# One row per token for the expert outputs: written by the first expert, accumulated by the second, with a last stage that reads half and gate/up weights in one transfer

## The reference, cut to what matters

```python
def hier_moe(h, w_coarse, b_coarse, w_fine, b_fine, w_gate, w_up, w_down):
    ...
    grp = jnp.argmax(pg_all, axis=-1)
    ...
    top_v, top_i = lax.top_k(fine, TOP_K)
    pe = jax.nn.softmax(top_v, axis=-1) * pg[:, None]
    ...
    a = (jax.nn.silu(jnp.einsum('td,edf->tef', t, w_gate))
         * jnp.einsum('td,edf->tef', t, w_up) * gates[:, :, None])
    y = jnp.einsum('tef,efd->td', a, w_down)
...
    x = x + g2 * hier_moe(h2, w_coarse, b_coarse, w_fine, b_fine, w_gate, w_up, w_down)
...
        y_prompt = rmsnorm(yp, final_g)
```

## Time and profile before

| | us |
|---|---|
| median of 3 runs | 995.99 (995.22 to 996.94) |
| the profiled execution | 995.4 |
| its span | 993.4 |
| stage 6, 603 to 951 us of the span | 348 |
| last stage, 951 to 993 us | 42 |

### The profile page before, as it was taken

The page is one execution under the profiler, slowest core; times in us unless marked ns, Lnnn a source line. Parts: engine busy times, 40 slices in busy tenths (PEclk is TensorE's granted clock), DMA queues, the critical chain, the costliest instruction groups (busy, mean ns, idle before and its releaser), DMA issues. The chain is left out here.

```text
span 993.4 us, 11991 instructions
## 1 busy us (share of the span) xinstructions
PE 908.7 (91%) x4615; PEld 688.2 (69%) x4615; DVE 601.5 (61%) x828; ACT 388.0 (39%) x551; POOL 158.2 (16%) x103
## 2 busy tenths in 40 slices
PE   4799999999996999978999956999999999999946
PEld 3589888999984555437888844767676777767512
DVE  6753223132424666544588774787888878788528
ACT  6431111011104766512453323655555454555114
POOL 0000000000004910000110101233233332323100
PEclk9899999999995999999999965999999999999979
DMA  9535535311002300021222183799999999999177
GB/s 371 211 120 204 202 140 218 100 44 43 1 1 90 105 1 2 8 70 43 85 64 67 61 359 130 280 379 357 374 362 366 364 363 367 361 369 342 71 286 306
DMA packets 38261, 190.95 MB, mean 192 GB/s; under 512 B 9654, under 2 KB 10806, under 8 KB 22840
## 3 DMA queue, kind: packets, MB, share of 16 engines
q1 hardware_dynamic: 28844, 170.76, 45.9%
q0 software_dynamic: 9216, 18.89, 5.0%
q10 hardware_dynamic: 144, 0.52, 0.1%
HBM read 178.48 MB, written 26.35 MB: 206 GB/s over the span
## 5 line engine op out<-in xcount | busy, mean ns | idle before, releaser
L1755 DVE TENSOR_TENSOR gu_lo<-w_gu,gu_hi 128x2048 fp32r<-128x2048 f32 x64 | 146.1, 2286 | 47.6 <-ACT gu_hi L1673 47.5
L573 PE MATMUL PS<-h_hi,w_hi 128*128 128x384 f32 x432 | 148.2, 343 | 5.4 <-DVE h_lo L436 5.4
L577 PE MATMUL PS<-h_hi,w_lo 128*128 128x384 f32 x432 | 145.1, 336 | 0.0
L575 PE MATMUL PS<-h_lo,w_hi 128*128 128x384 f32 x432 | 145.1, 336 | 0.0
L1673 ACT ACTIVATE gu_hi<-w_gu 128x2048 fp32r<-128x2048 f32 x64 | 122.0, 1907 | 19.8 <-PEq L1022 11.9
L1922 PE MATMUL PS<-gu_hi,xT_hi 128*128 128x512 f32 x256 | 116.6, 455 | 2.7 <-DVE xT_lo L1761 2.7
L1955 PE MATMUL PS<-w_d,aT 128*128 128x512 f32 x256 | 115.2, 593 | 1.3 <-DVE yrows L1783 1.3
L1622 POOL DMA_INDIRECT y_rows<-yrows,tab x32 | 69.3, 2167 | 213.9 <-DVE yrows L1783 213.9
L1924 PE MATMUL PS<-gu_hi,xT_lo 128*128 128x512 f32 x256 | 102.5, 400 | 0.0
L1923 PE MATMUL PS<-gu_lo,xT_hi 128*128 128x512 f32 x256 | 101.5, 397 | 0.0
L573 PEld LDWEIGHTS PS<-h_hi,w_hi 128*128 128x128 f32 x432 | 81.8, 189 | 14.2 <-issue 11.0
(11 more groups left out here) (200 smaller groups left out, 1523.8 us busy)
## 6 DMA issues: line engine op xcount, KB each, us to landing
w_gu<-in_w_gu SPq DMA_DIRECT2D x64, 1024.0 KB, 10.7
w_d<-in_w_down SPq DMA_DIRECT2D x32, 1024.0 KB
wm<-in_w_mod SPq DMA_DIRECT2D x10, 2048.0 KB, 8.0
w_raw<-in_w_in SPq DMA_DIRECT2D x18, 512.0 KB, 8.7
yt<-y_rows SPq DMA_DIRECT2D x9, 1024.0 KB, 13.2
xt<-in_x_all SPq DMA_DIRECT2D x9, 512.0 KB, 3.5
y_all<-yt SPq DMA_DIRECT2D x9, 512.0 KB, 2.8
wmh<-in_w_mod SPq DMA_DIRECT2D x2, 2048.0 KB
```

The source lines that it names most:

```text
L573: pe.matmul(o, w_hi[b][:, k, :], h_hi[:, k, tok], start=k == 0, stop=False)
L575: pe.matmul(o, w_hi[b][:, k, :], h_lo[:, k, tok], start=False, stop=False)
L577: last = pe.matmul(o, w_lo[b][:, k, :], h_hi[:, k, tok], start=False, stop=k == KD - 1)
L1755: dve.tensor_tensor(gu_lo[:, n % 3, h, :], w_gu[:, n % 3, h, :], raw(gu_hi[:, n % 2, h, :]), ALU.subtract).then_inc(s_lo, 1)
```

## The change

`y_rows` has one row for each token. Of a token's two experts the one that comes first in the order of processing writes its row, the other adds to it with an accumulating DMA. For this the table's entries are no longer 2 * token + k + 1 but 2 * token + 1 for the first and 2 * token + 2 for the later one; which is later is found in `slots` by comparing the experts' numbers (`chosen`, plus 32 for each round of 128 places). `split_table` makes two lists of `tab`: `tabw`, where the later ones are out of bounds, and `taba`, where the first ones are. In the last stage 0.5 MiB is loaded for each tile; tiles 1, 3, 5 and 7 are added to the residual by PE alone, with an identity matrix, and their squares and scaling read PSUM; the other five by one DVE addition. The gate/up weights of an expert come in one transfer of 2 MiB, issued after the second half's products.

```diff
+            def final_rows(t):
+                return PS[:, 2 * (t // 2):2 * (t // 2) + 2, :] if t in PE_SUMS else halves(yt[:, t, :])
...
                     for n in range(NE):
                         if n + 3 < NE:
-                            for h in range(2):
-                                sp.wait_ge(s_gu, 2 * n + h + 1)
-                                load_gu(n + 3, h)
+                            sp.wait_ge(s_gu, 2 * n + 2)
+                            load_gu(n + 3)
...
                     def scatter(n):
                         pool.wait_ge(s_y, n + 1)
                         pool.indirect_dma_start(
                             out=y_rows, out_offset=bass.IndirectOffsetOnAxis(
-                                tab[:, n:n + 1].bitcast(U32), 0),
+                                tabw[:, n:n + 1].bitcast(U32), 0),
...
+                        if n >= 1:
+                            pool.wait_ge(s_out[(n - 1) % 2], 16 * ((n - 1) // 2 + 1))
+                        pool.indirect_dma_start(
+                            out=y_rows, out_offset=bass.IndirectOffsetOnAxis(
+                                taba[:, n:n + 1].bitcast(U32), 0),
+                            in_=yrows[:, n % 2, :], in_offset=None, bounds_check=T - 1,
+                            oob_is_err=False, compute_op=ALU.add).then_inc(s_acc[n % 2], 16)
...
                     def high(n, h):
-                        act.wait_ge(s_wgu[n % 3][h], 16 * (n // 3 + 1))
+                        act.wait_ge(s_wgu[n % 3], 16 * (n // 3 + 1))
...
                     def blend(n):
                         if n >= 2:
                             dve.wait_ge(s_out[n % 2], 16 * (n // 2))
+                            dve.wait_ge(s_acc[n % 2], 16 * (n // 2))
...
+                        dve.wait_ge(s_yt[t], 16)
+                        x = yt[:, t, :].rearrange("p (k n) -> p k n", k=KD)
+                        dve.tensor_tensor(x, x, cat[:, :, t * P:(t + 1) * P], ALU.add
                                           ).then_inc(s_x3, 1)
...
                     for t in range(NT):
-                        combine(t)
+                        if t not in PE_SUMS:
+                            combine(t)
                         if t:
                             finish(t - 1)
```

More of the change, by code:

```diff
@@ L126, in build @@
         with ExitStack() as same:
-            slotf, entry, tab, tabg, gtab, of_ctx, tabacc, count, gu_lo, w_d = later_buffers(same)
+            slotf, entry, tab, tabg, gtab, tabw, taba, of_ctx, tabacc, count, gu_lo, w_d = later_buffers(same)
         with ExitStack() as same:
-            for name, shape, dt in LATER[:8]:
+            for name, shape, dt in LATER[:10]:
                 allocator(same)(name + "_y", shape, dt)
-            yt = allocator(same)("yt", [P, NT, TOPK, D])
+            yt = allocator(same)("yt", [P, NT, D])
         with ExitStack() as same:
-            for name, shape, dt in LATER[:8]:
+            for name, shape, dt in LATER[:10]:
                 allocator(same)(name + "_w", shape, dt)
@@ L969, in build @@
         s_xclear = sem("s_xclear")
-        s_wgu = [[sem(f"s_wgu{i}_{h}") for h in range(2)] for i in range(3)]
+        s_wgu = [sem(f"s_wgu{i}") for i in range(3)]
         s_wd = [sem(f"s_wd{i}") for i in range(3)]
@@ L993, in build @@
             erm = sb4("erm", [P, 2, NE])
-            cmax, csum, grp, v0, v1, ex, e01 = [sb4(f"per_tile{i}", [P, NT]) for i in range(7)]
+            cmax, csum, grp, v0, v1, ex = [sb4(f"per_tile{i}", [P, NT]) for i in range(6)]
+            chosen = sb4("chosen", [P, TOPK, NT])
+            turn_of = sb4("turn_of", [P, TOPK, 3], I32)
+            order = sb4("order", [P, TOPK, 3])
             gates = sb4("gates", [P, TOPK, NT])
@@ L1258, in choose @@
                                           ).then_inc(s_rdve, 1)
-                        for k in range(TOPK):
-                            link(dve.tensor_tensor(entry[:, k, tiles, 0, :], oh[k][:, tiles, :],
-                                                   spread(row_id[:, k, tiles], NE), ALU.mult))
                     def slots(t0, n):
@@ L1277, in slots @@
                         dve.sem_inc(s_within, 1)
+                        tiles = slice(t0, t0 + n)
+                        turns, later_of = turn_of[:, :, 0:n], order[:, :, 0:n]
+                        link(dve.tensor_copy(turns, slotf[:, :, tiles]))
+                        link(dve.tensor_scalar(turns, turns, 7, 5, ALU.logical_shift_right,
+                                               ALU.logical_shift_left))
+                        link(dve.tensor_tensor(chosen[:, :, tiles], chosen[:, :, tiles], turns,
+                                               ALU.add))
+                        for k in range(TOPK):
+                            link(dve.tensor_tensor(later_of[:, k, :], chosen[:, k, tiles],
+                                                   chosen[:, 1 - k, tiles], ALU.is_gt))
+                        link(dve.tensor_tensor(later_of, later_of, row_id[:, :, tiles], ALU.add))
+                        for k in range(TOPK):
+                            link(dve.tensor_tensor(entry[:, k, tiles, 0, :], oh[k][:, tiles, :],
+                                                   spread(later_of[:, k, :], NE), ALU.mult))
                     def weigh(t0, n):
@@ L1358, in _ @@
                                       ).then_inc(s_tab, 1)
+                    split_table(0)
                     dve.tensor_tensor(gtab[:], PS[:, 7, TABLE + NE:TABLE + 2 * NE],
@@ L1512, in build @@
         s_store = sem("s_store")
+        s_acc = [sem(f"s_acc{i}") for i in range(2)]
         LAP = (NE + 2) // 3
-        DVE_SUMS = (0, 4)
-        PE_SUMS = [t for t in range(NT) if t not in DVE_SUMS]
+        TABS = 8
+        PE_SUMS = (1, 3, 5, 7)
         with ExitStack() as st:
@@ L1737, in _ @@
                         act.wait_ge(s_out[b], 16 * NE // 2)
+                        act.wait_ge(s_acc[b], 16 * NE // 2)
                     for t in range(NT):
@@ L2031, in _ @@
                         pe.wait_ge(s_yt[t], 16)
-                        if t >= 4:
-                            pe.wait_ge(s_x3, t - 3)
                         for half in range(2):
-                            for k in range(TOPK):
-                                last = pe.matmul(PS[:, 2 * (t % 4) + half, :], ident[:],
-                                                 yt[:, t, k, half * 512:half * 512 + 512],
-                                                 start=k == 0, stop=k == TOPK - 1)
+                            o = PS[:, 2 * (t // 2) + half, :]
+                            pe.matmul(o, ident[:], yt[:, t, half * 512:half * 512 + 512],
+                                      start=True, stop=False)
+                            last = pe.matmul(o, ident[:], cat[:, 4 * half:4 * half + 4,
+                                                              t * P:(t + 1) * P],
+                                             start=False, stop=True)
                         last.then_inc(s_sum, 1)
```

117 lines of the change are left out of this document (71 added, 46 removed).

## The result

The changed kernel took 1017.93 us (median of 4 runs, 1015.71 to 1020.71), the kernel before beside it 996.12 us (995.22 to 996.94). The ratio is 1.022, with a 95% interval of 1.019 to 1.025. The prediction was 1000.5 us with a range up to 1016.0, so it had the sign right and the size wrong, and the time lies above its range.

The account below looks back on a forecast made before the run. In stage 6 PE sets the pace, with the DMA engines busy 97%, also near their limit. Terms -10.8 + 1.8 + 3.5 + 10 = +4.5 on 995.4 give 999.9, plus 0.6 for the median 1000.5 us; range 988.5 to 1016.

Parts of the forecast that it names:

- Stage 6, weights in one transfer: Gate/up loads in stage 6: issued later as one transfer, costing nothing alone; 0 taken, best case 0.16 us per step gained.
- slack of 0.9 us: Stage 6: DVE's product is ready at 721.5, PE wants it at 722.4; this margin was subtracted once.
- POOL and DVE's waits: Stage 6: POOL's wait for the previous write and `blend`'s wait for the accumulation of n-2 cost nothing.
- Last stage: Final stage from SP's first load: 31.2 us instead of 42.0, -10.8 us, bounds -9 to -12.
- Routing: Before the first gather: added routing and `split_table` operations delay stage 6 by 3.5 us, bounds 2.5 to 4.5.
- Last scatter: After expert 31's write: POOL issues the accumulation, which also reads the old row; +1.8 us, bounds 1.3 and 4.5.
- Accumulation: Stage 6: reading 36 old rows costs the DMA engines 0.385 us a step; +10 us, bounds 0 to +21.
- the DMA engines have room: Stage 6 rival: old-row reads fit the free 0.26 us, steps stay 10.13 us; 990.5 us, chance 0.30.
- the accumulation is dear: Stage 6 rival: each accumulated row costs a DMA engine a latency; above 1012 us, chance 0.12.
- two prices: Stage 6, latency per accumulated row: half of 2.2 us gives some +60, 1055 us; a fifth gives 1015.
- two signs: Stage 6 signs of dear accumulation: `blend` waits for accumulations; the indirect queue's share exceeds 14.5% + 4%.
- The list of what would show each step: Signs expected in the profile: last stage 31 us, last scatter 1.8 later, first gather 3.5 later, stage 6 steps 10.4 us.

Follow-up runs that it names:

- a1: Kernel before with an expert's gate/up weights in one 2 MiB transfer with 16 KB rows, all else old; 1002.6 us, ratio 1.0074.
- a2: Changed kernel with gate/up weights back in two 1 MiB transfers with 8 KB rows; 1002.07 us.
- h1: Kernel before with both weight halves asked for late, when the second half of the buffer is free, still two transfers; 995.5 us, ratio 0.9996.
- h2: Kernel before with one 2 MiB weight transfer per expert, asked for late, reading 8 KB pieces; 1002.7 us, ratio 1.0069.
- g1: Changed kernel with a third buffer for the experts' output rows, so blend waits for the accumulation of three experts ago; 1017.9 us.
- f1: Changed kernel with weights in halves and each gather issued ahead of POOL's wait for the product; 1001.8 us, ratio 1.0063.
- g3: Changed kernel with a third buffer for output rows and each gather issued ahead of POOL's wait for the product; 1015.0 us.
- a4: Changed kernel with weights in two transfers of 8 KB rows and the second scatter a plain write, addition left out; 990.5 us.
- b2: Changed kernel with the single 2 MiB weight transfer laid out in 4 KB pieces instead of 16 KB; 1022.1 us.
- b1: Changed kernel with the single 2 MiB weight transfer laid out in 8 KB pieces instead of 16 KB; 1013.0 us.
- c1: Changed kernel with weights in two 1 MiB transfers, both issued late where the single one is; 1012.2 us.

## Why the prediction was wrong, point by point

**The failed step** is *Stage 6, weights in one transfer*: "The cover is gone, but alone this costs nothing", with bounds from a gain of 0.16 us a step to 0. It measured 6.6 us alone (`a1` against before) and 15.9 in the changed kernel (after against `a2`). The loss alone comes from the one landing and not from the late issue: `h1` asks as late and takes 995.5 us, `h2` joins the landings and takes 1002.7. Three things are wrong in the step. It did not look at the start of the stage, where nothing else is queued and ACT can use the first half before the second is there; 3.9 of the 6.6 us are lost in the fill. In the middle it let the slack of 0.9 us be spent once, while in `a1` ACT waits 106.0 us for weights and PE's weight loads wait for the product in 16 of some 25 steps; the 31 steps take 2.6 us more. And it priced the single transfer by itself, while beside accumulations it made the steps 13.7 us longer (after against `a2`), with PE waiting for gathered rows and four times at the lower clock behind such a wait. The bounds had no loss in them, though the text itself said that the slack was being used up. A step that removes cover has a bound above zero, from what is late next. With the two halves put back the total is near: the prediction gave 1000.5 and `a2` took 1002.1. Its parts agree less well, since the last scatter took 4.2 us where 1.8 were counted.

**A second step failed with it:** *POOL and DVE's waits* rested on a landing of 9.9 us, with 14.3 at hand. With the single transfer the accumulations of the chain took 14.0 to 17.5 and the writes 15.0, so all the waits that it priced at 0 came. DVE's wait for the accumulation is worth some 6 us of the steps (`g1`), POOL's place nothing beside halves (`f1`). What PE's own waits for gathered rows cost with the single transfer no run separates, since `g3`, which was to take them away, left them.

*Last stage:* -11.2 against -10.8; its working held. `a4`, `a2` and after give 31.9, 31.2 and 30.8.

*Routing:* +2.9 against 3.5; in kernels with the routing of before the first gather stood at 603.5 to 606.0, in those with the new one at 607.5 to 609.6, so the term is 4 us to within 1. Its bounds were 2.5 to 4.5.

*Last scatter:* +4.5 against 1.8. Both bounds were right and the choice was wrong: 1.3 is what a plain second scatter costs (`a4`, 4.6 against 3.3), and the read took a whole landing again (7.5 to 7.8). "The DMA engines are idle there" was no reason for the low end: at a DMA share of 0.23 (960 to 980 us of after) the accumulation landed after 6.36 us and the plain scatter after 3.21.

*Accumulation:* +10 against 8.6 (31 steps of `a2` and `a4`, both with halves); the fill is 37.8 us in both. The 0.385 us a step were 0.37. That the slack of 0.9 is used up in the first steps was wrong: 16 steps passed first, then each cost 0.64. That the sum is near all the same is partly luck.

*The rivals.* That the DMA engines have room: refuted in `a2` and after; `a4`, which leaves the addition out, takes 990.5 us, the rival's number. That the accumulation is dear, a latency for each row: refuted by 0.37 us a step. (By its own terms its two prices come to some 1059 and 1017 us instead of 1055 and 1015.) Of its two signs one came, `blend` waiting for accumulations (27.7 us), and the other did not: the indirect queue's share is 17.5% and not over 18.5%. The rule of the page Collectives: The Full Stack of the Trainium skill (The bandwidth ceiling), that a reducing transfer costs its second read, agrees with the 0.37. The list of what would show each step asked for a DMA share of 0.98 or more beside steps of 10.4 us; it was 0.93 beside steps of 10.6 on average, and that should have been named as the sign of a third case: long steps while neither PE nor the DMA engines are full, hence waits.

## What to carry to other kernels

Price the joining of two transfers also at the place where nothing else is queued, for what can no longer start before all has landed: in `a1` 3.9 of the 6.6 us were lost there, while asking late with two landings cost nothing in the whole (`h1`). Where an engine and the DMA queues are both near their limit, edits don't add (11.6 and 10.5 us apart made 27.4), so bound each beside the others and test the square. Look at the granted clock beside PE's waits: behind long ones it fell, and an estimated 6.8 of the 22.3 us were lost there while PE was busy. And read the chain of waits as one path of several that are as long: a third buffer removed the ring that it showed, made the steps 6.1 us shorter and the kernel no faster.

## What the runs showed of the hardware that I had not expected

- The size of a plain transfer's pieces moves the landings of both queues. Beside 4, 8 and 16 KB pieces of weights, gathers landed in 10.4, 15.3 and 14.4 us and the weights in 14.4, 11.7 and 10.6 (`b2`, `b1`, after); without accumulations gathers in 11.5 (8 KB) and 15.7 (16 KB). With 8 KB pieces in two transfers (`c1`) they were 13.7 and 14.4, so the size alone doesn't decide it.
- Four times in the steps of after PE waited 1.9 to 3.0 us and then had a granted clock of 0.50, where its eight matmuls of `down` took 5.13 us instead of 3.44.
- An indirect scatter in which most of 128 entries are skipped costs nothing that can be measured in a full stage with weights in halves: 306.4 us for 31 steps with it and without it. It costs 1.3 us when it is the last, and 3.3 in the steps beside the single transfer.
- An accumulation into DRAM with no loads beside it lands after 6.36 us, a plain scatter after 3.21. In a full stage with halves it takes 0.37 us a step of the DMA engines, where the bytes that it reads come to 0.385.
- DVE's 128x1024 addition takes 3.37 us instead of 1.23 while POOL adds in SBUF, and DVE's scaling with one input in PSUM keeps its 1.28 us.
